# One run of weight groups through the even layer, norms one stage later, and both attentions in blocks of two heads

## What is computed

```python
# layer 0 (even)
h = rmsnorm(x, even_norm_mix)
dn_qkv, dn_a, dn_b, dn_gate, fq, fk, fv = split_cols(h @ even_w_in)
dn_qkv = silu(causal_dwconv(dn_qkv, even_dn_conv))        # 4 taps
o_a = gated_deltanet(...)            # 4 heads of 128, chunks
o_a = rmsnorm(o_a, even_dn_norm) * silu(dn_gate)
o_b = softmax(q1 k1^T) v - lam * softmax(q2 k2^T) v       # 4 heads, rotary, 2 x 64, block-causal
o_b = rmsnorm(o_b, even_diff_subln) * (1 - lam_init)
x = x + concat(o_a, o_b) @ even_w_out
x = x + conv_gated_mlp(rmsnorm(x, ffn_norm[0]))           # width 2816
# layer 1 (odd)
o_c = chunk_band_attention(...)      # 16 heads of 64, relative bias, softmax
x = x + o_c @ odd_w_out
x = x + conv_gated_mlp(rmsnorm(x, ffn_norm[1]))
return rmsnorm(x, final_norm)
```

## Time and profile before

| | |
|---|---|
| Runs | 1452.70, 1458.46, 1458.87 us (median 1458.46) |
| Profiled execution | 1460.56 us, its span 1458.9 us |
| TensorE busy | 1391.2 us (95% of the span) |
| VectorE busy | 843.6 us (58%) |
| ScalarE busy | 619.7 us (42%) |
| GpSimd busy | 181.2 us (12%) |
| Mean granted TensorE clock | 0.964 |

### The profile page before, as it was taken

One profiled execution on the slowest core, in us unless ns is written; L12 is line 12 of the kernel. 1 busy time (PEld: TensorE's weight loads), 2 busy tenths in 40 slices (PEclk: granted clock), 3 DMA queues, 4 the chain that ended last, 5 costly groups with the idle time before them and its releaser, 6 DMA issues.

```text
span 1458.9 us, 19831 instructions
## 1 busy us (share of the span) xinstructions
PE 1391.2 (95%) x6775; PEld 1138.7 (78%) x6775; DVE 843.6 (58%) x1235; ACT 619.7 (42%) x865; POOL 181.2 (12%) x177
## 2 busy tenths in 40 slices
PE   5979999899989999999999999999999999999996
PEld 4769878677767888888888777777778888888874
DVE  5666675566655666435555556667556664355542
ACT  4333232355543444223334566666444442233342
POOL 1031033011222100000001312122220000000011
PEclk9979979899989999999999999999999999999998
DMA  6421011012323642333313422324223323334132
GB/s 190 147 58 30 20 39 30 15 44 58 115 58 102 171 131 73 107 108 92 110 54 90 129 71 82 89 70 112 76 58 98 103 72 107 109 87 114 55 90 58
DMA packets 218642, 124.80 MB, mean 86 GB/s; under 512 B 6048, under 2 KB 215435, under 8 KB 218341
## 3 DMA queue, kind: packets, MB, share of 16 engines
q1 hardware_dynamic: 213744, 112.54, 27.4%
q0 software_dynamic: 3664, 11.58, 2.8%
q10 hardware_dynamic: 1188, 0.08, 0.1%
HBM read 119.94 MB, written 9.48 MB: 89 GB/s over the span
## 4 chain that ended last, share of the span: by engine, by line
PE 86%; DVE 5%; ACT 5%; issue 3%; DMA 1%; POOL 0%; ACTq 0%; DVEq 0%; SPq 0%; POOLq 0%
PE acc L619 24%; PE acc L620 23%; PE acc L621 23%; PE R L720 4%; ACT wh L373 2%; PE R L874 2%; PE R L863 1%; PE R L846 1%; PE R L658 1%; PE R L847 1%; PE R L740 1%; DVE wl L377 1%; DVE cta L1362 1%; PE R L718 1%; DMA xin<-in_x 1%
## 5 line engine op out<-in xcount | busy, mean ns | idle before, releaser
L619 PE MATMUL acc<-mh,wh 128*128 128x512 f32 x1120 | 456.4, 408 | 9.5 <-DVE ml L1315 5.4
L621 PE MATMUL acc<-mh,wl 128*128 128x512 f32 x1120 | 442.0, 395 | 0.0
L620 PE MATMUL acc<-ml,wh 128*128 128x512 f32 x1120 | 441.4, 394 | 0.0
L377 DVE TENSOR_TENSOR wl<-raw,wh 128x2048 fp32r<-128x2048 f32 x116 | 251.8, 2171 | 135.8 <-ACT wh L373 135.7
L373 ACT ACTIVATE wh<-raw 128x2048 fp32r<-128x2048 f32 x116 | 210.1, 1811 | 145.7 <-PE acc L621 144.3
L619 PEld LDWEIGHTS acc<-mh,wh 128*128 128x128 f32 x1120 | 213.9, 191 | 56.0 <-issue 9.2
L621 PEld LDWEIGHTS acc<-mh,wl 128*128 128x128 f32 x1120 | 213.1, 190 | 46.2
L620 PEld LDWEIGHTS acc<-ml,wh 128*128 128x128 f32 x1120 | 214.0, 191 | 41.5 <-issue 2.6
L494 POOL TENSOR_TENSOR ssum<-ssum,sq 128x512 f32<-128x512 f32 x32 | 52.0, 1624 | 716.8 <-ACT sq L1007 716.1
L619 PE MATMUL acc<-ah,wh 128*128 128x512 f32 x352 | 137.7, 391 | 0.4 <-DVE wl L377 0.3
L621 PE MATMUL acc<-ah,wl 128*128 128x512 f32 x352 | 137.0, 389 | 0.0
(11 more groups left out here) (285 smaller groups left out, 1780.5 us busy)
## 6 DMA issues: line engine op xcount, KB each, us to landing
raw<-in_ffn_w_in SPq DMA_DIRECT2D x88, 512.0 KB, 5.0
raw<-in_even_w_in SPq DMA_DIRECT2D x24, 512.0 KB, 5.2
raw<-in_ffn_w_out SPq DMA_DIRECT2D x32, 384.0 KB, 4.1
raw<-in_ffn_w_out SPq DMA_DIRECT2D x32, 320.0 KB, 3.6
raw<-in_odd_w_qkv SPq DMA_DIRECT2D x16, 512.0 KB, 4.5
rel_bias_extended<-rel_bias_rows POOLq DMA_DIRECT2D x16, 320.0 KB, 4.0
raw<-in_even_w_out SPq DMA_DIRECT2D x8, 512.0 KB, 4.6
raw<-in_odd_w_qkv SPq DMA_DIRECT2D x16, 256.0 KB, 3.1
```

Of the source, the lines that this page charges most:

```text
L377: nc.vector.tensor_tensor(wl[s][:, 0:n], raw[s][:, 0:n], wh[s][:, 0:n].bitcast(F32), ALU.subtract).then_inc(sem(f"w_tail{s}"), 1)
L619: nc.tensor.matmul(o, ah_, bh_, start=first, stop=False)
L620: nc.tensor.matmul(o, ah_, bl_, start=False, stop=False)
L621: return nc.tensor.matmul(o, al_, bh_, start=False, stop=last)
```

## The change

- **One sequence of weight groups.** In the even layer the slots now go by pair: first q and k of both heads (slot 0 and slot 1), then v and gate of both. Only the 32 groups of q and k of pair 0 (and a, b) run before pair 0. All later groups, through the four attention heads to the output projection, are one generator, of which `give` takes a number at each place, and `upto` gives up to a count (`AHEAD = 8` groups of the next unit at each head's end).
- **Postponed norms.** The sums of squares and the spread of a DeltaNet pair run inside the next pair (or the first attention head), those of an attention head in part in the next head; the output waits in `os`, or in `osb`.
- **Masks.** `C_STRICT` goes into the constant masks; GpSimd's masks of `decT`, `decN` and the copies `gC` go, one mask of `qkD` comes.
- **Attentions.** Query and key keep head and tail in separate full tiles (`qs`, `ks`), and each block of both halves is six matmuls over 64 rows each. Four exponential buffers; the difference is written over the first exponential with no division by its sum (the sum enters the norm's epsilon); odd transposes in fewer groups; all value products in one run at the end.
- The differential heads are four copies of straight code, and the last 28 groups of the output projection can run in the last head.

```diff
-                        w = slice(0, (b + 1) * P)
-                        nc.tensor.matmul(r[:, w], qs[m][:, b * P:(b + 1) * P], kh[m][:, w], start=True, stop=False)
-                        done(nc.tensor.matmul(r[:, w], qs[m][:, b * P:(b + 1) * P], kl[m][:, w], start=False,
-                                              stop=True), ph, f"s{t}", i)
+            def scores(ph, i, b, n):
...
+                for step, (x_, y) in enumerate(((0, 0), (0, 1), (1, 0))):
+                    for m in (0, 1):
+                        ins = nc.tensor.matmul(r[m][:, w], qs[x_][half[m], b * P:(b + 1) * P], ks[y][half[m], w],
+                                               start=(step == 0), stop=(step == 2))
```

```diff
+            def diff_head(i, fill):
...
+                scores(ph, 0, 0, i)
+                give(fill, 4)
+                if i:
+                    diff_rows(i - 1)
+                else:
+                    post_rows(1)
+                scores(ph, 0, 1, i)
+                give(fill, 4)
+                values(ph, 0, UNIT["diff"] + i, vf)
+                turned(0)
+                scores(ph, 0, 2, i)
+                give(fill, 4)
+                turned(1)
+                scores(ph, 0, 3, i)
+                give(fill, 4)
+                turned(2)
+                if i < NH - 1:
+                    rope_products(i + 1)
+                give(fill, 3)
+                turned(3)
+                give(fill, 3)
+                o = job(ph, "pv", 0)
...
+            fill = chained(dn_units(1), dn_units(2), dn_units(3), *(attn_units(UNIT["diff"] + i) for i in range(NH)),
+                           out_terms(out0, (range(6), (6,)), heads_wait, 1))
+            dn_pair(0, fill)
+            upto(fill, 68)
+            dn_pair(1, fill)
+            upto(fill, 120 + AHEAD)
+            post_sums(1)
+            for i in range(NH):
+                diff_head(i, fill)
+                if i < NH - 1:
+                    upto(fill, 120 + 24 * (i + 1) + AHEAD)
```

VectorE's order in a differential head, and at the start of the even layer:

```diff
+                minima(3)
...
+                difference(3)
...
+                if i < NH - 1:
+                    rope(i + 1)
+                    units_split_dve(dve, 0, UNIT["diff"] + i + 2)
+                    both_tails("diff", i + 1)
+                    value_evac(vf, UNIT["diff"] + i + 1, (ph, "vt", 0))
...
+            first = qk_evac(0)
+            for _ in range(4):
+                next(first, 0)
             r = full(dve, "ab", "abT", 0)
             free(V.tensor_copy(abs_[:, :], r[0:8, :]), "ab", "abT", 0)
-            for _ in first:
-                pass
+            for _ in range(2):
+                next(first, 0)
```

More of the change, by code:

```diff
@@ L48 @@
 ALPHA = 4
+TURNED = [P * b * (b + 1) // 2 for b in range(NB)]
+AHEAD = 8
 LINE = 40
@@ L511, in _ @@
             for p in range(NH // 2):
[L512 to L524, removed]
+                ph = f"dn{p}"
                 for h in (0, 1):
@@ L777, in dn_pair @@
                     last = "X" + w
-                step("u", "U", "vb", [last, "vtok"])
-                step("wT", "kbg", "U", ["ktok"])
+                pe.wait_ge(sem("silu"), TURN[2 * p + 1, 2] + 1)
+                step(two, "vtok", "vT", None)
+                step(two, "u", "U", "vb", [last, "vtok"])
+                step(two, "wT", "kbg", "U", ["ktok"])
                 o = []
@@ L892, in attn_units, with rope_products @@
-            def attn_units(g):
-                return both(features(0, g, (mh, ml)), features(1, g, (mh, ml), tiles=1))
-            def out_terms(base, heads, last, srcwait):
-                for s in (0, 1):
-                    begin(s, base)
-                    ws = [w[s][:, :].rearrange("p (t k n) -> p t k n", t=2, k=KD) for w in (wh, wl)]
-                    for t in (0, 1) if s == 0 else (0,):
+                    give(fill, 1)
+            def rope_products(i):
+                ph = f"diff{i - 1}" if i else "rope"
+                for n, nm_ in enumerate(("rot_q", "rot_k")):
+                    pe.wait_ge(sem("acc_free0"), 2 * (i + UNIT["diff"]) + n + 1)
+                    r = job(ph, nm_, 0)
+                    done(nc.tensor.matmul(r[:, :], cblk(C_PERM), qr[n][:, :], start=True, stop=True), ph, nm_, 0)
@@ L1154, in _ @@
+            first = qk_evac(0)
+            for _ in range(3):
+                next(first, 0)
             act.wait_ge(sem("ab_in"), 1)
@@ L1235, in _ @@
-            rest_split_act(act)
-            attention("diff", NH - 1, NH, iter(()), more=False)
+                settled(act, is_full("odd", "pv", i))
+                A(dyn(oh, i), R[3][:, :], ACT.Copy).then_inc(sem("o_head"), 1)
+                next(evac, 0)
+            for i in range(NH):
+                diff_head(i)
+            diff_gain(NH - 1)
+            diff_round(NH - 1)
             def out_proj(base, norm):
@@ L1435, in beta, with dn_pair, piece @@
+            def dn_pair(p, evac, pieces):
+                ph = f"dn{p}"
                 def beta(h):
                     return ball[:, 2 * p + h, :]
+                def piece(at):
+                    for _ in range(pieces.get(at, 0)):
+                        next(evac, 0)
                 for h in (0, 1):
@@ L1725, in attention @@
+                for b in range(NB):
+                    minima(b)
+                    if b == 2:
+                        next(evac, 0)
+                    normalise(b)
+                for _ in range(4):
+                    next(evac, 0)
+                full(dve, "odd", "pv", i)
+                dve.wait_ge(sem("o_head"), i + (NH + 1))
+                free(V.tensor_tensor(dyn(ol, i), R[3][:, :], dyn(oh, i).bitcast(F32), ALU.subtract), "odd", "pv", i)
                 next(evac, 0)
```

1202 lines of the change are left out of this document (640 added, 562 removed), and 7 rows, old and new, of the table _DN.

## The result

The changed kernel took 1465.95 us (median of 7 runs, 1463.7 to 1467.97), the kernel before 1458.50 us beside it. The ratio is 1.0066, 95% interval 1.0039 to 1.0092: slower by 0.7%, where 1446 and a gain had been forecast. The range (1422 to 1468) held the time, the sign was wrong. That it held is luck: its upper end came from rival B, whose mechanism did not come about. The profiled execution has a span of 1463.5 us.

The account below looks back on a forecast made before the run. TensorE bounds the odd pairs; the even mixers are a TensorE, VectorE and ScalarE chain. Up to the first head -11, heads +8.7, scores -1, odd pairs -8.8: -12.1 from 1460.6, 1448.5 profiled, 1446 us median; range 1422 to 1468.

Parts of the forecast that it names:

- rival B: Scores: row tiles run one behind the other, +21 us against the forecast, 1467 us; chance 0.18.
- Start of the even layer: Before the gates: with 32 groups moved behind, TensorE idles some 10 us against 7.7, gates start at 68; +2.3 us.
- Wait ahead of the first head, -4.5: Before the first differential head: eight groups ahead and the rotation moved into the last block cover the wait; -4.5 us.
- DeltaNet norms, -4.8: Ends of DeltaNet pairs 0 and 1: postponing the norms removes 2.4 us of waiting at each; -4.8 us.
- Fill, clock, boundary, recurrence, together -4: DeltaNet pairs: denser fill -5, less slow clock -5, late convolution between pairs +4, thinner cover in pair 0's recurrence +2 us.
- rival C: Covers hold: clock stays up, pair 1 loses all waits, pair boundary costs nothing, head's wait 3 us; 1425 us, chance 0.17.
- rival D: Even layer gains nothing: stands at the start and between the pairs bring the same slow stretches; 1456 us, chance 0.20.
- The upper bound of the whole sum, +6: Up to the first head: the terms sum to -11 us, with bounds -26 and +6.
- The heads' wait of 5.3 us: Three differential heads: groups behind the rotation products wait for slot 0's tail, split on VectorE only after the rotation; +16 us.
- The other terms of the heads, -7.3: Differential heads: waits at the end of three heads gone, -6.3 us; value products in one run, -1 us.
- Odd pairs, -1.1 each: Eight odd pairs: value products in one run, fewer transpose groups, short copy waits gone; -1.1 us each, -8.8 in all.
- Scores, -1 in 12 units: Score matmuls: six half-row passes run in pairs, 3.0 us per unit including entry and exit against 3.1; -1 us over 12 units.

Follow-up runs that it names:

- the run with the norms at once: Changed kernel with the DeltaNet pairs' output norms computed at each pair's own end again, one sequence of groups kept: 1467.14 us, ratio 1.0068 to the kernel before.
- the early split: Changed kernel with slot 0's weight split moved ahead of score block 3 in the first three differential heads: 1447.73 us, ratio 0.9958 to the kernel before.
- the three edits together: Changed kernel with slot 0 split early, value transposes in bank 3, and the odd output projection's fourth tile kept back: 1432.54 us, ratio 0.9839.
- The whole-row run: Changed kernel with four score products over all 128 rows per block instead of six over 64, scores not the reference's: 1456.36 us, ratio 1.001.
- the stacked operands: Early split, values' bank and odd tile kept back, plus odd pairs' scores over whole rows as in the kernel before: 1430.84 us, ratio 0.9819.

## Why the prediction was wrong, step by step

The forecast was -12.1 us for the whole execution. The medians give +7.5, the profiled spans +4.6, and the parts from the first group to the last, which can be compared term by term, +8.5.

- **Start of the even layer**: right. The gates' start was forecast at 68; it is 65.6 in a run whose groups start 2.0 us earlier. Counted with the 32 groups moved behind it, it costs 1.7 us where 2.3 were charged.
- **Wait ahead of the first head, -4.5**: right; it is gone, in the run with the norms at once as well.
- **DeltaNet norms, -4.8**: right in sign, mis-sized. Postponing saves 7.9 us in the new order; at pair 1's end it is the 2.4 of the forecast, between the pairs 7.1, because norms at once would stand behind ScalarE's other work there. What postponing alone would be worth in the old order no run shows. That head 0 would pay for them was missing: 37.7 us against 34.7, of which 1.7 is the spread itself and the rest a stretch at half clock.
- **Fill, clock, boundary, recurrence, together -4**: about -6 by what is left of the 16.9, without a run of its own. Pair 1 runs without a stand and at full clock, which was rival C's claim. The slow stretches behind a stand remain: clock 0.80 for 17.4 us and 0.73 for 25.7, 3.5 and 6.9 us lost where the prediction read 4.4 and 3.9, so the -5 put on them did not come; that was rival D's claim. TensorE stands 2.3 us between the pairs. (The upper bound of the whole sum, +6, is added wrongly: its terms give +7.7. Nothing hangs on it.)
- **The heads' wait of 5.3 us**: right in place and releaser, 4.84, 4.84 and 5.19. Its price was taken at its length, with "the clock has its stand as before": the early split shows 15.7 us for the three, half as much again as the length it takes away. That 15.7 agrees with the +16 of the forecast is luck: the forecast is three stands of 5.3 us without the clock, the run three reductions by 3.4 with it. The other terms of the heads, -7.3, are matched by the 7.3 us of the three edits together. What the heads missed, 4.3 us, is the bank of the next step (5.0 in heads 0 to 2).
- **Odd pairs, -1.1 each: the step that failed.** The forecast listed "short waits for the copies of the transposed blocks" as gone and looked for a new one only at the minima of block 0. The new order of TensorE puts the value transposes and the first exponential transposes next to each other, and the lists of jobs by bank (`DIFF_JOBS`, `ODD_JOBS`) left both in one bank. That is about 1 us in each of 12 units, and 12 to 14.5 us by the run that takes it away; with that alone the ratio is 0.9982, no change. One odd pair, 25.61 us before and 26.09 after, can be split by runs: 24.22 with neither the wait nor the half rows (-1.4, where -1.1 was forecast), +0.95 for the half rows, +0.92 for the wait at the bank.
- **Scores, -1 in 12 units**: a mis-sized term. The products of both halves do run side by side, 3 ns apart, so rival B is false, although its time (1467) is the nearest. But a unit's blocks take about 3.5 us instead of 3.0, since a visit to half rows costs 0.4 to 0.5 us and not 0.25. The whole-row run puts the difference at 8 to 10 us in all and 0.70 a pair, the stacked operands at 0.95 a pair. The prediction also said that no matmul over part of the rows is in the trace. There are four over 8 rows (L703, 45.82 us): 0.32 us lead into them instead of 0.23, and the group behind them starts with 0.34 instead of 0.23, the same signature as at the half rows. The Trainium skill, TensorEngine Tiling, Key Properties, has both halves of this, tiles that work independently and a drained array at a change of mode; the trace agrees with the first, and has 0.4 us or more at each change, which fits the second but does not show that draining is what takes the time.
- **Output projections**: no term at all, +3.8 and about +4.5. "None is added or removed" was true of the groups and said nothing of what they covered. In the odd layer the cause is shown (3.35 us of it won back), in the even layer only argued.

From -12.1 to +8.5: DeltaNet -5.9, heads 0 to 2 +4.3, head 3 +1.1, even projection +3.8, odd pairs 0 to 6 +10.3, last pair and its projection +6.1, scores (counted within these) +1. The DeltaNet's extra gain of 5.9 hid part of the miss.

## What to carry to other kernels

When work that waited on another engine is merged or moved, write down for every PSUM bank who writes it next and who must have read it first: a neighbour in the same bank costs a full read by the other engine at each pass. The bank may have been shared all along: the profile of before shows nothing of it while other work lies between the two, so ask what lies there after the move. An experiment that undoes one part of a change undoes it within the new order: look at its trace for a stand that neither kernel had before its difference is called that part's worth. Price a stand of TensorE with the slow clock behind it, here half as much again as the stand itself. A split of the array pays only if it saves more passes per visit than the visit costs: here one pass of at most 0.23 us was bought for 0.4 or more.

## What the runs showed of the hardware that was not expected

- The order in which products of two row halves are issued does not matter within a block of six: the first product of rows 64 to 127 started 10 ns after the first of rows 0 to 63, though two others were issued between them.
- After a stand of 4.8 us the granted clock is at half for the next matmuls (0.43 us from start to start instead of 0.23); with stands of some 1.3 us per head (the three edits together) it stays at 1.00 through the whole head.
- A subtraction of 64 rows by 512 columns on VectorE took 1.67 and 1.65 us when it began while one of GpSimd's was under way, and 0.68 when both began together (stacked operands, pair 0 and the later pairs).
